# Second dense block of a two-block transformer kernel: four gate halves move from the attention's steps to the scans, and the weight ring gets two more slots

## The chip, the core and the metric

The kernel runs on one core of a Trainium2 chip. The metric is the device time of one execution in microseconds (us), the median of several runs. The engines of the core are TensorE (PE; its weight loads are PEld), VectorE (DVE), ScalarE (ACT), GpSimd (POOL) and SyncE (SP), which in this kernel issues nearly all transfers of weights. Everything is in 32-bit floats.

## The reference

256 tokens of width 1024 go through two blocks. The first is a mixer with three branches and a mixture of 32 experts. The second, in which the change lies, is:

```
def hybrid_layer(x, mem, ...):               # the second block, cut
    h = rms_norm(x, g_mix)
    u, q, k, v, qi, ki, wi, qm, gates = split(h @ w_in)
    y_ssm = s5_branch(u, ...)                # scan over 256 positions, gelu, y * sigmoid(y @ w_glu)
    y_dsa = dsa_branch(q, k, v, qi, ki, wi)  # attention on the keys that an index score picks
    y_mem = memory_branch(qm, km, vm)        # attention on the memory
    g_s, g_d, g_m = split(sigmoid(gates))    # 3 x 1024 columns of w_in
    merged = g_s*(y_ssm@w_up_ssm) + g_d*(y_dsa@w_up_dsa) + g_m*(y_mem@w_up_mem)
    x = x + merged @ w_out
    return x + hier_moe(rms_norm(x, g_ffn), ...)   # 32 experts, 2 of one group for each token
```

Each expert of `hier_moe` has three matrices, w_gate and w_up (1024 x 512) and w_down (512 x 1024), 2 MB each. The kernel reads all of them.

## The kernel before

Each engine has its program, written out in order by hand (`tensor`, `vector`, `scalar`, `sync`, `gpsimd`), and the engines meet by semaphores. `pe["name"]`, `dve["name"]`, `act["name"]` are the counts at which a named step is done.

**Weights.** The ring is a tile of seven slots of 2 MB. `fetcher` (L287 on) issues the transfers of SP: each call takes the next slot of its `lane`, waits until the weight that the slot holds has been read (`pe["free", ...]`), and issues. SP works in order, so a fetch that waits holds up all behind it. In the second dense block all weights go by the lane `d2 = (0, 1, 2)`; slots 3 to 6 hold work of the state space branch (tables, scans). Then come the 96 weights of the second mixture, in eight rounds `u` of four experts: four w_gate, four w_up, four w_down, on the lane (3, 4, 5, 6, 0, 1, 2). They wait for `sy 3` (the last product of the scans' states), and the fourth for `branch 2,0` (the output of the state space branch), since it takes slot 6.

**Gates.** The gate columns are six weights `c` of 512 columns; a gate half `i` (`gate_half`, L544 on) is four products of 128x128 by 128x512, half of the sum of one block of 128 tokens: `c = i // 4`. ACT takes a finished pair out of PSUM by a tanh (`scalar_gate`).

**The attention's steps.** `tensor_dense2` runs a loop over `s` from 0 to 13 (L958 on): `scores(s)`, `turn_p` of step s - 2, a gate half for s below 9, `values(s - 2)`. DVE does in each step the softmax, its weights, a copy of the values and one piece of `scan_step(0, s)`.

**The scans.** `driven(c)` makes the inputs of scan c (0 to 3) on PE, `scans(c)` runs it on DVE, `states(c)` multiplies its states out, `skip(c)` adds the skip term. `up(n, h)` multiplies branch n by half h of its up weight, in two parts (token blocks) in PSUM banks 0, 1 and 6, and `gated(n, h)` on DVE multiplies by the gate and frees the bank. DVE's order is scans(1), skip(0), scans(2), skip(1), gated(2,0), gated(2,1), scans(3), skip(2), gated(1,0), skip(3), gated(1,1). Behind skip(3) come the gelu (`yg`), `glu`, `branch 2,0`, up(0,0), up(0,1), the merge, its transposes (`mt2`), w_out, the norm, and the router.

**The second mixture.** `tensor_route` waits for four small loads of router weights (`s_r2`), which ACT's queue issues behind the attention's loop. `tensor_moe2` does in a round: the w_gate group (64 matmul rows of the trace, all four experts), the w_up group, spread of the round before, gather of the next, transposes (`at2`), the w_down group. A group waits for its four weights.

Work tiles lie in one large tile `ar`. GMo (offset 19024) up to 23120 holds gain vectors, masks and the memory's keys and values; 6736 to 10832 holds branch outputs and, in the mixture, selection matrices, sigmoids and outputs.

Of the kernel before, what the change touches and what calls it, by code (L numbers as in the profile page):

```python
# [8 lines left out]
ALU = mybir.AluOpType  # L9
# [5 lines left out]
NSLOT = 7  # L15
# [3 lines left out]
NE = 32  # L19
# [90 lines left out]
def build(nc, a, out, ctx):  # L110
# [11 lines left out]
    ring = ctx.enter_context(nc.sbuf_tensor("ring", [128, NSLOT * SLOT], F32))  # L122
# [22 lines left out]
    def pair(blk, u):  # L145
# [6 lines left out]
        10832, 12880, 14928, 16976, 19024, 20048, 21072, 22096, 23120, 23760, 23888)  # L152
    XV, XNV, YV = A(X, 2, 1024), A(XN, 2, 1024), A(Y, 2, 1024)
# [85 lines left out]
    TOP, NM, SM = A(10224, 2, 8), A(10240, 2), A(10242, 2)  # L239
    CT, SEL = A(10256, 256, part=(0, 32)), A(10512, 2, 32)  # L240
# [61 lines left out]
    def sync(q):  # L302
# [405 lines left out]
    def tensor_route(t, w, m, W, n, cap):  # L708
# [19 lines left out]
        w.sums(b[:, 0:32], [(upper, SEL[:, 0, :])])  # L728
        w.sums(b[:, 32:64], [(upper, SEL[:, 1, :]), (ones, SEL[:, 0, :])])
        pe["rk", m] = w.sums(b[:, 64:96], [(ones, SEL[:, 0, :]), (ones, SEL[:, 1, :])])  # L730

    def gather(t, w, m, u, lane):
        b = w.claim("swt", m, u, lane=lane)
        t.wait_ge(s_dve, dve["sel", m, u])
        for i in range(2 if m == 1 else 1):
            for tb in range(2):
                ins = t.e.transpose(b[:, TB(2 * i + tb)], SWB[:, i, tb, :], ident)  # L737
        pe["swt", m, u] = t(ins)
        t.wait_ge(s_act, act["rows", m])
        for h in range(2):  # L740
            b = w.claim("hg", m, u, h, lane=lane)
            for k in range(4):
                pe["hg", m, u, h, k] = w.sums(b[:, TB(k)], [(XNV[:, tb, TB(4 * h + k)], SB[u % 2][:, tb, :])
                                                           for tb in range(2)])

    def spread(t, w, m, u, lane):
        def block(i):
            t.wait_ge(s_act, act["yg", m, u, i])
            for tb in range(2):
                for h in range(2):  # L750
                    b = w.claim("sp", m, u, i, tb, h, lane=TL1X if i else lane)
                    pe["sp", m, u, i, tb, h] = w.sums(b[:, :], [(SWT[u % 2][:, i, TB(tb)], YG_[i][:, HALF(h)])])
# [112 lines left out]
    def tensor_dense2(t, w):  # L865
# [92 lines left out]
        for s in range(14):  # L958
# [4 lines left out]
            if s < 9:  # L963
# [36 lines left out]
        states(2)  # L1000
# [13 lines left out]
    def tensor_moe2(t, w):  # L1014
# [3 lines left out]
        for u in range(NE // 4):  # L1018
            HG, AT_ = HGB[u % 2], ATB[u % 2]
# [521 lines left out]
    def vector_ranks(v, m, cap):  # L1541
        v(v.own.tensor_scalar(SEL, CMB, 0.0, None, ALU.not_equal))
# [8 lines left out]
        v(v.own.scalar_tensor_tensor(out=RK, in0=rk, scalar=1.0, in1=SEL, op0=ALU.add, op1=ALU.mult))  # L1551
# [9 lines left out]
    def vector_select(v, m, u):  # L1561
# [14 lines left out]
        else:  # L1576

            four = [z[:, :, 4 * u:4 * u + 4].unsqueeze(3).to_broadcast([128, 2, 4, 32]) for z in (RK, CMB)]
            S = SB[u % 2].rearrange("p b (x s) -> p b x s", x=4)
            v(v.own.tensor_tensor(S, iota[:, 0:32].unsqueeze(1).unsqueeze(1).to_broadcast([128, 2, 4, 32]), four[0],  # L1580
                                  ALU.is_equal))
            k = v(v.own.tensor_tensor(SWB[:, 0].rearrange("p b (x s) -> p b x s", x=4), S, four[1], ALU.mult))
# [85 lines left out]
    def vector_dense2(v):  # L1668
# [254 lines left out]
    def vector_moe2(v):  # L1923
# [39 lines left out]
        for u in range(NE // 4):  # L1963
            sg = TM[0][:, 0:512]
# [216 lines left out]
    def scalar_gather(s, m, u, l1):  # L2181
# [4 lines left out]
        s(s.own.activation(SWT[u % 2][:, 0:n, :], ps("swt", m, u)[:, 0:256 * n].rearrange("p (i q) -> p i q", i=n),  # L2186
# [62 lines left out]
    def scalar_dense2(s):  # L2249
# [59 lines left out]
        for k in range(14):  # L2309
# [21 lines left out]
        scalar_mt(s, 2)  # L2331
        for tb in range(2):
            root_block(s, "h4", tb, dve["x3", tb, 1], YV)

    def scalar_moe2(s):
# [12 lines left out]
        for u in range(NE // 4):  # L2348
# [3 lines left out]
            act["sg2", u] = s(s.own.activation(TM[0][:, 0:512], ps("w_gate_2", u)[:, :], ACT.Sigmoid))  # L2352
# [127 lines left out]
```

## Time and profile before

| | before |
|---|---|
| median of 3 runs | 2299.73 us (2291.16 to 2302.4) |
| the profiled execution | 2301.27 us, span in the trace 2299.4 us |
| PE busy | 1850.2 us (80%), 11518 instructions |
| DVE busy | 807.2 us (35%) |
| ACT busy | 497.7 us (22%) |
| DMA | 713.56 MB, mean 310 GB/s |
| mean granted TensorE clock | 0.915 of full speed |

The first block and the first mixture take the span up to about 1475 us, the second dense block reaches to about 1820, and the second mixture is the rest. Shares are averages over all of these. The time from 2299.4 to 2301.27 lies around the traced span.

### The profile page before, as it was taken

To read this page: it belongs to the slowest core of one execution; us is meant where nothing else is said; L and a number is where in the kernel's file an instruction comes from. 1 tells how busy PE (TensorE), PEld (TensorE's weight loads), DVE (VectorE), ACT (ScalarE), POOL (GpSimd) and SP (SyncE) were. 2 spreads that over 40 slices of the span, in tenths; PEclk is the share of its full clock that TensorE was granted. 3 is DMA by queue.
4 is the path that set the end of the run, shared out by engine and by line. 5 is a ranking of instruction groups with operands and counts; after the bars stand their busy time and mean duration, and the time that the engine had idled before them with its cause. 6 is when DMAs were issued, how large, how long until landed. Compare 5 with 4: busy or idle time off the path is not lost. (4 is left out here: it accounts for less than half of the span.)

```text
span 2299.4 us, 28288 instructions
## 1 busy us (share of the span) xinstructions
PE 1850.2 (80%) x11518; PEld 837.1 (36%) x11518; DVE 807.2 (35%) x1624; ACT 497.7 (22%) x1008; POOL 77.8 (3%) x96
## 2 busy tenths in 40 slices
PE   7899998888988989779887898699977755565555
PEld 3655545333333333333333333254534422222221
DVE  2224333333433244442444433587583300000001
ACT  2031302222232133331333323321301200000000
POOL 0000000000000000000000000084000000000000
PEclk9999999899999989999999999899998877877877
DMA  7744358497797699998999999633125399999996
GB/s 270 272 162 155 120 197 326 200 380 319 323 398 309 273 424 389 423 424 341 379 424 423 424 424 421 219 128 133 40 74 219 142 428 428 428 427 428 427 427 263
DMA packets 113956, 713.56 MB, mean 310 GB/s; under 512 B 16703, under 2 KB 21006, under 8 KB 68654
## 3 DMA queue, kind: packets, MB, share of 16 engines
q1 hardware_dynamic: 105344, 704.98, 75.5%
q10 hardware_dynamic: 8398, 5.47, 0.8%
q8 instruction: 166, 2.72, 0.5%
q14 instruction: 48, 0.39, 0.1%
HBM read 709.35 MB, written 1.07 MB: 309 GB/s over the span
## 5 line engine op out<-in xcount | busy, mean ns | idle before, releaser
L795 PE MATMUL ps<-ring,ar 128*32 128x512 f32 x3072 | 380.9, 634 | 47.6 <-DMA ring<-in_w 26.1
L436 PE MATMUL ps<-ar 128*128 128x128 f32 (+5 forms) x1750 | 360.1, 363 | 36.3 <-PEq L706 15.4
L443 PE MATMUL ps<-ring,ar 128*32 128x512 f32 x1536 | 208.2, 704 | 194.1 <-DMA ring<-in_w_up 82.2
L436 PEld LDWEIGHTS ps<-ar 128*128 128x128 f32 (+2 forms) x1750 | 236.1, 201 | 161.0 <-issue 111.1
L436 PE MATMUL ps<-ring,ar 128*128 128x512 f32 (+2 forms) x624 | 268.0, 590 | 15.5 <-DVE ar L1889 8.9
L795 PEld LDWEIGHTS ps<-ring,ar 128*32 128x32 f32 x3072 | 100.2, 114 | 324.8 <-issue 277.6
L1645 DVE TENSOR_SCALAR ar<-ps 128x256 f32<-128x256 f32 x128 | 54.3, 424 | 443.5 <-PE ps L795 436.6
L806 PE MATMUL ps<-ring,ar 128*32 128x512 f32 x1536 | 175.1, 595 | 21.7 <-ACT ar L2244 21.7
L443 PEld LDWEIGHTS ps<-ring,ar 128*32 128x32 f32 x1536 | 60.0, 127 | 336.3 <-issue 335.4
L436 PEld LDWEIGHTS ps<-ring,ar 128*128 128x128 f32 x624 | 120.6, 195 | 155.9 <-issue 137.6
L551 PE MATMUL ps<-ring,ar 128*128 128x512 f32 x384 | 172.4, 598 | 0.0
L1591 DVE TENSOR_TENSOR ar<-ps,ar 128x512 f32<-128x512 f32 x180 | 124.5, 692 | 100.2 <-PE ps L436 91.4
L2216 ACT ACTIVATE ar<-ps 64x512 f32<-64x512 f32 x256 | 151.5, 592 | 26.1 <-PE ps L806 14.3
L2210 ACT ACTIVATE ar<-ar 128x256 f32<-128x256 f32 x128 | 53.3, 417 | 385.2 <-DVE ar L1645 382.4
L1653 DVE TENSOR_TENSOR ar<-ar 128x256 f32<-128x256 f32 x128 | 79.3, 620 | 119.8 <-ACT ar L2210 109.7
L2244 ACT ACTIVATE ar<-ps 128x256 f32<-128x256 f32 x128 | 49.2, 384 | 239.5 <-PE ps L816 218.0
L551 PEld LDWEIGHTS ps<-ring,ar 128*128 128x128 f32 x384 | 71.2, 192 | 78.1 <-issue 77.7
L1966 DVE TENSOR_TENSOR ar<-ps,ar 128x512 f32<-128x512 f32 x8 | 5.5, 692 | 266.7 <-ACT ar L2352 266.7
L788 PE MATMUL ps<-ar 32*32 32x512 f32 x384 | 53.7, 622 | 49.5 <-ACT ar L2216 19.3
L806 PEld LDWEIGHTS ps<-ring,ar 128*32 128x32 f32 x1536 | 46.4, 109 | 114.6 <-issue 90.2
L2193 ACT ACTIVATE ar<-ps 128x512 f32<-128x512 f32 x80 | 47.8, 597 | 104.1 <-PE ps L436 104.1
L2186 ACT ACTIVATE ar<-ps 128x512 f32<-128x512 f32 (+1 forms) x40 | 22.2, 555 | 179.7 <-PE ps L737 177.6
(392 smaller groups left out, 1285.9 us busy)
## 6 DMA issues: line engine op xcount, KB each, us to landing
ring<-in_w SPq DMA_DIRECT2D x192, 2048.0 KB, 18.4
ring<-in_w_gate SPq DMA_DIRECT2D x32, 2048.0 KB, 17.8
ring<-in_w_up SPq DMA_DIRECT2D x32, 2048.0 KB, 16.7
ring<-in_w_down SPq DMA_DIRECT2D x32, 2048.0 KB, 16.0
ring<-in_w_in SPq DMA_DIRECT2D x21, 2048.0 KB, 8.7
ring<-in_w_ada SPq DMA_DIRECT2D x12, 2048.0 KB, 8.8
ring<-in_w_out SPq DMA_DIRECT2D x4, 2048.0 KB, 8.1
ring<-in_w_branch SPq DMA_DIRECT2D x6, 1024.0 KB, 5.0
```

The costliest lines, as they stand in the source:

```text
L436: ins = self.t.e.matmul(o, l, r, start=(i == 0), stop=(i == len(pairs) - 1))
L443: ins = self.t.e.matmul(b[32 * i:32 * i + 32, :], l, r, start=(k == 0), stop=(k == len(steps) - 1))
L551: ins = t.e.matmul(b[:, :], HV[:, k, TB(tb)], W[:, k, :], start=(k == 0), stop=(k == 7))
L788: e.matmul(b[32 * s:32 * s + 32, :], pick, B1R[:, HALF(s)], start=True, stop=False)
L795: ins = e.matmul(b[32 * s:32 * s + 32, :], HG[:, 2 * c + r, 32 * n:32 * n + 32], W[:, r, HALF(s)], start=False, stop=(c == 3 and r == 1))
L806: ins = e.matmul(b[64 * h + 32 * r:64 * h + 32 * r + 32, :], AT_[:, 2 * s + r, 32 * n:32 * n + 32], W[:, s % 2, r, HALF(h)], start=(s == 0 ...
L1591: v(v.own.tensor_tensor(o, ps("sp", m, u, i, tb, h)[:, :], o, ALU.add))
L1645: dve["glu", u, n] = v(v.own.tensor_scalar(glu, b[:, 0:512:2], 7.0, None, ALU.min))
L1653: dve["ac", u, n] = v(v.own.tensor_tensor(o, lin.rearrange("p (q r) -> p q r", r=2), sg.rearrange("p (q r) -> p q r", r=2), ALU.mult))
L2210: act["sg", u, n] = s(s.own.activation(M[:, 512:768], M[:, 0:256], ACT.Sigmoid, scale=1.702))
L2216: k = s(s.own.activation(YG_[n // 2][64 * (n % 2):64 * (n % 2) + 64, HALF(h)], ps("l2", u, n)[64 * h:64 * h + 64, :], ACT.Copy))
L2244: m = s(s.own.activation(o, ps("at", u, k)[:, 256 * i:256 * i + 256].rearrange("p (r s n) -> p r s n", r=2, s=4), ACT.Copy))
```

## The change

Three things go together. Four gate halves (16 to 19) leave steps 5 to 8 of the loop, and all of 16 to 23 stand between the scans' products. The weights of the block and of the mixture get nine slots: slot 7 is GMo to 23120, slot 8 is 6736 to 10832 of `ar`. For that the mixture's small tiles move, AT and SWT get homes of their own (AT2 is single), the lanes are set weight by weight, and SP's order changes: the up weights go out behind `pv 11`, w_out behind three w_gate. The router's loads go behind the transposes of the merge on ACT's queue, as their tile now lies in a gate's place, and gated(1,0) goes behind skip(3).

```diff
-NSLOT = 7
+NSLOT = 9
+RING = 7
@@ def RG_(i, off, *shape):
+        if i >= RING:
+            return A(MORE[i - RING] + off, *shape)
@@
+    MORE = (GMo, 6736)
@@ tiles of the mixture
-    AC2 = A(4096, 512)
+    AT2, AC2, YG2 = A(2048, 4, 128), A(3072, 512), A(3584, 1024)
+    SB2 = [A(4608 + 256 * i, 2, 128) for i in range(2)]
+    SWB2 = A(5120, 1, 2, 128)
+    SWT2 = [A(5376 + 256 * i, 1, 256) for i in range(2)]
+    SG2 = A(5888, 512)
@@
-    W36, B36 = A(9216, 8, 36), A(9504, 36)
+    W36, B36 = A(2512, 8, 36), A(2800, 36)
@@ def sync(q):
         for c in range(6):
             fetch(("gate", 2, c), w_in2[:, :, 1988 + 512 * c:2500 + 512 * c], 8, 512, lane=d2)
-        for n in (2, 1):
-            for h in range(2):
-                up(n, h)
-        fetch(("glu",), kpn(a["w_glu_2"][0]), 4, 512, lane=d2)
-        for h in range(2):
-            up(0, h)
-        for h in range(2):
-            fetch(("wo", 2, h), kpn(a["w_out_2"][0])[:, :, HALF(h)], 8, 512, lane=d2)
+        up(2, 0, (1,))
+        q.wait_ge(s_pe, pe["pv", 2, 11])
+        up(2, 1, (7,))
+        up(1, 0, (2,))
+        up(1, 1, (0,))
+        fetch(("glu",), kpn(a["w_glu_2"][0]), 4, 512, lane=(1,))
+        up(0, 0, (7,))
+        up(0, 1, (2,))
+        units = [(nm, u, i) for u in range(NE // 4) for nm in ("w_gate_2", "w_up_2", "w_down_2") for i in range(4)]
+        lanes = (3, 4, 5, 6, 8, 7, 2, 0, 1)
         q.wait_ge(s_pe, pe["sy", 3])
-        for u in range(NE // 4):
-            for nm, r in (("w_gate_2", 8), ("w_up_2", 8), ("w_down_2", 4)):
-                for i in range(4):
-                    if (u, nm, i) == (0, "w_gate_2", 3):
-                        q.wait_ge(s_dve, dve["branch", 2, 0])
-                    fetch((nm, u, i), a[nm][0, 4 * u + i].rearrange("(p r) n -> p r n", r=r), r, SLOT // r,
-                          lane=(3, 4, 5, 6, 0, 1, 2))
+        for k, (nm, u, i) in enumerate(units):
+            if k == 3:
+                out2(0, (0,))
+                out2(1, (1,))
+                q.wait_ge(s_dve, dve["branch", 2, 0])
+            if k == 4:
+                q.wait_ge(s_pe, pe["up", 0, 1, 1])
+            r = 4 if nm == "w_down_2" else 8
+            fetch((nm, u, i), a[nm][0, 4 * u + i].rearrange("(p r) n -> p r n", r=r), r, SLOT // r,
+                  lane=(lanes[k % 9],))
@@ def tensor_dense2(t, w): the loop over s
-            if s < 9:
+            if s < 5:
                 gate_half(t, w, 2, 11 + s)
@@ and behind it
         driven(1)
         states(0)
-        gate_half(t, w, 2, 20)
-        gate_half(t, w, 2, 21)
+        for i in (16, 17):
+            gate_half(t, w, 2, i)
         driven(2)
-        gate_half(t, w, 2, 22)
-        gate_half(t, w, 2, 23)
+        for i in (18, 19, 20, 21):
+            gate_half(t, w, 2, i)
+        states(1)
+        driven(3)
+        for i in (22, 23):
+            gate_half(t, w, 2, i)
         t.wait_ge(s_dve, dve["branch", 2, 2])
         up(2, 0, side)
-        states(1)
-        driven(3)
         up(2, 1, side)
+        states(2)
         t.wait_ge(s_dve, dve["branch", 2, 1])
         up(1, 0, side)
-        states(2)
         states(3)
         up(1, 1, side)
@@ def vector_dense2(v):
         scans(3)
         skip(2)
-        gated(1, 0)
         skip(3)
         dve["tc"] = v.n
+        gated(1, 0)
         gated(1, 1)
@@ def scalar_dense2(s): in the loop over k, and behind it
-            if k < 10 and k % 2 == 0:
+            if k < 5 and k % 2 == 0:
                 scalar_gate(s, 2, 5 + k // 2)
-        e.dma_start(W36[:, :, 0:4], kpn(a["w_group_2"][0])).then_inc(s_r2, 16)
...
-        got["rt", 2] = 64
-        for g in range(10, 12):
+        for g in range(8, 12):
             scalar_gate(s, 2, g)
...
         scalar_mt(s, 2)
+        e.dma_start(W36[:, :, 0:4], kpn(a["w_group_2"][0])).then_inc(s_r2, 16)
...
+        got["rt", 2] = 64
@@ def scalar_moe2(s):
-            if u > 1:
-                s.wait_ge(s_pe, pe["l2_2", u - 2, 1])
-            act["at2", u] = s(s.own.activation(ATB[u % 2][:, 0:4, :],
+            if u > 0:
+                s.wait_ge(s_pe, pe["l2_2", u - 1, 1])
+            act["at2", u] = s(s.own.activation(AT2,
```

## Rows read from the trace of the kernel before

**Rows 1.** The page: DMA's busy tenths and GB/s in 40 equal slices.

```profile
DMA  7744358497797699998999999633125399999996
GB/s 270 272 162 155 120 197 326 200 380 319 323 398 309 273 424 389 423 424 341 379 424 423 424 424 421 219 128 133 40 74 219 142 428 428 428 427 428 427 427 263
```

**Rows 2.** Chain of waits in order of time: start, us, piece.

```profile
1828.95 7.12 PE ps L443 x64
1836.08 7.57 DMA ring<-in_w_up
...
2277.45 8.77 PE ps L443 x64
```

**Rows 3.** A window: busy us by engine, TensorE clock, DMA share, GB/s.

```profile
1860.00:2260.00 400.00, 222.93 (x1568) 85.48 (x1572) 32.84 (x49) 25.60 (x45) 0.00 (x0) 0.78 1.01 427
```

**Rows 4.** Timeline of SP's issues: start, us, tensor, count.

```profile
1758.51 2.21 SPq L296 DMA_DIRECT2D ring<-in_w_gate  x4
1801.56 34.85 SPq L296 DMA_DIRECT2D ring<-in_w_up  x4
```

**Rows 5.** Timeline of PE, attention steps (L936 starts a step, L551 gate half).

```profile
1620.50 0.70 PE L936 MATMUL ps<-ar 64*128 64x256 f32 x4
...
1622.54 3.60 PE L551 MATMUL ps<-ring,ar 128*128 128x512 f32 x8
...
1645.41 0.70 PE L936 MATMUL ps<-ar 64*128 64x256 f32 x4
...
1648.39 0.66 PE L954 MATMUL ps<-ar 128*64 128x128 f32 x8 [0.78 <-DVE small L1395]
1648.98 0.70 PE L936 MATMUL ps<-ar 64*128 64x256 f32 x4
...
1654.15 0.60 PE L568 MATMUL ps<-ar 128*128 128x128 f32 x4
```

**Rows 6.** Timeline of PE, last attention step to states(3).

```profile
1661.74 2.11 PE L436 MATMUL ps<-ring 32*128 32x256 f32 x16
1663.78 3.22 PE L443 MATMUL ps<-ring 128*32 128x256 f32 x32
1666.93 7.13 PE L551 MATMUL ps<-ring,ar 128*128 128x512 f32 x16
...
1704.59 13.64 PE L436 MATMUL ps<-ring,ar 128*128 128x512 f32 x24 [8.90 <-DVE ar L1889]
...
1731.98 3.25 PE L443 MATMUL ps<-ar,ring 128*32 128x256 f32 x32 [11.89 <-DVE ring L1880]
```

**Rows 7.** Timeline of DVE, weights of step 10, gated(2,.), next turn_in.

```profile
1651.98 0.74 DVE L1397 TENSOR_SCALAR ar<-ar,small 128x256 f32<-128x256 f32 x2
...
1703.84 2.23 DVE L1889 SCALAR_TENSOR_TENSOR ar<-ar,ps 128x512 f32<-128x512 f32 x3
1711.40 0.69 DVE L1889 SCALAR_TENSOR_TENSOR ar<-ar,ps 128x512 f32<-128x512 f32 x1 [5.33 <-PE ps L436]
1712.12 0.69 DVE L1823 TENSOR_TENSOR ar<-ps,ring 128x512 f32<-128x512 f32 x1
```

**Rows 8.** Windows at the end of the attention steps.

```profile
1656.00:1660.00 4.00, 2.24 (x20) 1.29 (x16) 3.52 (x9) 1.26 (x5) 0.00 (x0) 0.95 0.00 0
1656.00:1672.00 16.00, 13.55 (x88) 7.07 (x85) 13.43 (x21) 1.80 (x5) 0.00 (x0) 0.79 0.10 12
```

**Rows 9.** DMA issues: KB of each, median us to landing.

```profile
ring<-in_w_out SPq DMA_DIRECT2D x4, 2048.0 KB, 8.1
...
ar<-in_w_router ACTq DMA_DIRECT2D x1, 128.0 KB, 15.9
...
ar<-in_w_expert ACTq DMA_DIRECT2D x1, 128.0 KB, 2.6
```

**Rows 10.** Timeline of PE, w_out and the router's sums.

```profile
1771.22 22.56 PE L436 MATMUL ps<-ring,ar 128*128 128x512 f32 x48 [2.28 <-ACT ar L2106]
...
1801.37 1.87 PE L436 MATMUL ps<-ar 128*128 128x36 f32 x16
```

More of the change, by code:

```diff
@@ L235, in build @@
     TM = [A(9216 + 768 * i, 768) for i in range(2)]
[L236 removed]
+    AT2, AC2, YG2 = A(2048, 4, 128), A(3072, 512), A(3584, 1024)
[3 more added lines that the diff above has]
+    SG2 = A(5888, 512)
     B1R = A(HT, 2048, part=(0, 32))
     L, E, E2 = A(10000, 2, 32), A(10064, 2, 40), A(10144, 2, 40)
[L239 to L240 removed]
+    TOP, NM, SM = A(10224, 2, 8), small[:, 104:106], small[:, 106:108]
+    CT, SEL = A(10256, 256, part=(0, 32)), [A(10512, 2, 32), A(2872, 2, 32)]
     AT = [A(2048 * i, 8, 256) for i in range(2)]
@@ L727, in tensor_route @@
         t.wait_ge(s_c2, 16)
-        w.sums(b[:, 0:32], [(upper, SEL[:, 0, :])])
-        w.sums(b[:, 32:64], [(upper, SEL[:, 1, :]), (ones, SEL[:, 0, :])])
-        pe["rk", m] = w.sums(b[:, 64:96], [(ones, SEL[:, 0, :]), (ones, SEL[:, 1, :])])
+        s0, s1 = (SEL[m - 1][:, tb, :] for tb in range(2))
+        w.sums(b[:, 0:32], [(upper, s0)])
+        w.sums(b[:, 32:64], [(upper, s1), (ones, s0)])
+        pe["rk", m] = w.sums(b[:, 64:96], [(ones, s0), (ones, s1)])
     def gather(t, w, m, u, lane):
@@ L742, in gather @@
             for k in range(4):
-                pe["hg", m, u, h, k] = w.sums(b[:, TB(k)], [(XNV[:, tb, TB(4 * h + k)], SB[u % 2][:, tb, :])
+                pe["hg", m, u, h, k] = w.sums(b[:, TB(k)], [(XNV[:, tb, TB(4 * h + k)], (SB, SB2)[m - 1][u % 2][:, tb, :])
                                                            for tb in range(2)])
@@ L751, in block @@
                     b = w.claim("sp", m, u, i, tb, h, lane=TL1X if i else lane)
-                    pe["sp", m, u, i, tb, h] = w.sums(b[:, :], [(SWT[u % 2][:, i, TB(tb)], YG_[i][:, HALF(h)])])
+                    pe["sp", m, u, i, tb, h] = w.sums(b[:, :], [((SWT, SWT2)[m - 1][u % 2][:, i, TB(tb)],
+                                                            (YG_[i] if m == 1 else YG2)[:, HALF(h)])])
         block(0)
@@ L1018, in tensor_moe2 @@
         for u in range(NE // 4):
-            HG, AT_ = HGB[u % 2], ATB[u % 2]
+            HG, AT_ = HGB[u % 2], AT2
             rows = [slice(32 * i, 32 * i + 32) for i in range(4)]
@@ L1541, in vector_ranks @@
     def vector_ranks(v, m, cap):
-        v(v.own.tensor_scalar(SEL, CMB, 0.0, None, ALU.not_equal))
+        v(v.own.tensor_scalar(SEL[m - 1], CMB, 0.0, None, ALU.not_equal))
         dve["sel", m] = v.n
@@ L1550, in vector_ranks @@
         v(v.own.tensor_tensor(CO_, CO_, CMB, ALU.mult))
-        v(v.own.scalar_tensor_tensor(out=RK, in0=rk, scalar=1.0, in1=SEL, op0=ALU.add, op1=ALU.mult))
+        v(v.own.scalar_tensor_tensor(out=RK, in0=rk, scalar=1.0, in1=SEL[m - 1], op0=ALU.add, op1=ALU.mult))
         v(v.own.tensor_scalar(RK, RK, -1.0, None, ALU.add))
@@ L1578, in vector_select @@
             four = [z[:, :, 4 * u:4 * u + 4].unsqueeze(3).to_broadcast([128, 2, 4, 32]) for z in (RK, CMB)]
-            S = SB[u % 2].rearrange("p b (x s) -> p b x s", x=4)
+            S = SB2[u % 2].rearrange("p b (x s) -> p b x s", x=4)
             v(v.own.tensor_tensor(S, iota[:, 0:32].unsqueeze(1).unsqueeze(1).to_broadcast([128, 2, 4, 32]), four[0],
                                   ALU.is_equal))
-            k = v(v.own.tensor_tensor(SWB[:, 0].rearrange("p b (x s) -> p b x s", x=4), S, four[1], ALU.mult))
+            k = v(v.own.tensor_tensor(SWB2[:, 0].rearrange("p b (x s) -> p b x s", x=4), S, four[1], ALU.mult))
         dve["sel", m, u] = k
@@ L2185, in scalar_gather @@
             s.wait_ge(s_pe, pe["sp", m, u - 2, n - 1, 1, 1])
-        s(s.own.activation(SWT[u % 2][:, 0:n, :], ps("swt", m, u)[:, 0:256 * n].rearrange("p (i q) -> p i q", i=n),
+        s(s.own.activation((SWT, SWT2)[m - 1][u % 2][:, 0:n, :], ps("swt", m, u)[:, 0:256 * n].rearrange("p (i q) -> p i q", i=n),
                            ACT.Copy))
@@ L2351, in scalar_moe2 @@
                 s.wait_ge(s_dve, dve["ac2", u - 1])
-            act["sg2", u] = s(s.own.activation(TM[0][:, 0:512], ps("w_gate_2", u)[:, :], ACT.Sigmoid))
+            act["sg2", u] = s(s.own.activation(SG2, ps("w_gate_2", u)[:, :], ACT.Sigmoid))
             if u + 1 < NE // 4:
@@ L2364, in scalar_moe2 @@
                 s.wait_ge(s_pe, pe["l2_2", u, h])
-                n = s(s.own.activation(YG_[0][:, HALF(h)], ps("l2_2", u, h)[:, :], ACT.Copy))
+                n = s(s.own.activation(YG2[:, HALF(h)], ps("l2_2", u, h)[:, :], ACT.Copy))
                 read["l2_2", u, h] = s.mark()
```

26 lines of the change are left out of this document (14 added, 12 removed).

## The prediction, made before the changed kernel ran

> **What bounds the kernel now.** I read the page first, then the chain of waits from 1450 us on, then the timeline of each engine through the second dense block. The page's last fifteen slices [rows 1] fall into two parts: from slice 26 to 32 the DMA rate is low and uneven, and from slice 33 it stands at 427 to 428 GB/s. The chain [rows 2] shows what the second part is: in the second mixture every group of products waits for a weight (32 experts, three matrices of 2 MB, 96 transfers), so the end of the kernel is the time at which the stream of weights becomes continuous, plus the bytes that are left, plus a tail. One long window [rows 3] gives the rate, 427 GB/s, so one transfer of 2,097,152 bytes costs 4.91 us.
>
> When does the stream become continuous? The SP queue's timeline [rows 4] tells: four w_gate transfers go out at 1758.5, three w_up at 1801.6 as w_out and the last up weights leave slots 0 to 2, and then nothing, because seven slots are full. The eighth (w_up, expert 3) needs slot 3, which the first w_gate group reads. That group starts at 1828.95 and ends at 1836.0 [rows 2], and at 1836.08 SP goes on. From there 96 - 7 = 89 transfers are left, and the last group starts at 2277.45 [rows 2]: 441.4 us, of which 89 x 4.91 = 437.0 are bytes and 4.4 are start and landing. Then 22.0 us of tail to 2299.4. So two things move the end: the time of the first w_gate group (call it G), which the dense block's chain sets, and how many transfers are left at G.
>
> **Two more slots.** After the change nine slots are full at G: the lanes (3,4,5,6,8,7,2,0,1) take w_gate 0-3, w_up 0-3 and w_down 0. The last two go to slots 0 and 1 when the two w_out halves are read, in before's times at about 1794 and 1801.5 [rows 10], and 4.91 us each fit well before 1828.95. Left at G: 87. The gain is 2 x 4.91 = 9.8 us. It isn't given back later: with nine slots and 3 to 5 free per group the issues run further ahead than now, and now the window already shows a DMA share of 1.01 [rows 3]. The w_up group, which waits 7.57 us for its fourth weight today, starts at once; that only frees slots earlier. Bounds: nothing (if the stream slowed) and 9.8.
>
> A rule to weigh against this: the stream runs at 427 GB/s in the trace [rows 3]. The Trainium skill (DMA: Bandwidth & Descriptors, Where 436 GB/s comes from) says that HBM to SBUF is held to about 358 GB/s per core; by that rule, as an estimate, a transfer would cost 5.86 us and two slots would be worth 11.7. The trace decides, and it doesn't agree.
>
> **Four gate halves leave the attention's steps.** Loop s runs scores, turn_p, one gate half, values. From step 5 to 8 it takes 1620.50 to 1645.41, 24.91 us, with PE busy throughout [rows 5]: PE bound. Steps 9 and 10 have no gate half and take 3.57 us each (1645.41, 1648.98 and so on); of that 0.78 is PE waiting for ACT's copy of the turned weights, which a gate half of 3.44 us covers today [rows 5]. DVE's work in such a step fits: the weights that turn_p reads at 1654.15 are done at 1652.72 [rows 5, 7]. So steps 5 to 8 become 4 x 3.57, plus 0.39 in step 5 whose values (u = 3) are the longer kind: 14.7 us. Gain 10.2 us. ACT loses two gate evictions in the loop, which nobody waits for.
>
> **Where they land.** After the steps PE now runs driven(1), states(0), halves 16, 17, driven(2), 18 to 21, states(1), driven(3), 22, 23, up(2,0), up(2,1). Today DVE's scans bound this stretch, and PE has slack: it idles 8.9 us before 1704.59 [rows 6]. In before's times: 1666.93 when the first half starts; two halves 7.0 each pair [rows 6]. 1666.93 + 7.07 + 1.1 (driven) + 13.94 + 1.9 (states) + 1.1 + 6.97 = 1699.0; up(2,0) two parts to 1705.9, up(2,1) two parts to 1712.9. driven(2) keeps its place, so scans(2) isn't late. DVE reaches gated(2,0) at 1703.84 as now, follows PE's four parts, and the last ends at 1712.9 + 0.2 + 0.7 = 1713.8; scans(3) starts then, against 1712.12 now [rows 7]. Today DVE also waits here (5.33 us before 1711.40), because the fourth part needs a bank that DVE frees late and then runs at half clock after PE's idleness, 6.8 us instead of 3.5 [rows 6, 7]. So the 14 us that arrive cost only 1.7. Bounds: -0.6 if PE's slow start at 1661.74 (half clock, [rows 8], about 2.3 us) is gone, and 1.7 + 3.4 = 5.1 if one more half-clock stretch falls into this packed run (the one around 1660 is 6.7 us long: a mean of 0.79 over 16 us, [rows 8]).
>
> From scans(3) on, the order hardly changes. PE waits for DVE again (11.9 us before states(3) today [rows 6], some 11 after). gated(1,0) goes behind skip(3); skip(3) waits for states(3) in either case, and up(1,1)'s second part needs the bank that gated(1,0) frees only 3.4 us after its first has begun. Nought. G moves by -10.2 + 1.7 = -8.5.
>
> **Waits added on SP.** All weights of the block now queue behind pv 11; the first, up(2,1), lands some 5 us later and is wanted 40 us later. up(1,0), up(1,1), glu and up(0,.) each go out when their slot's user is done and land at least 8 us ahead of use. out2(0), out2(1) stand behind three w_gate: with wait sy 3 over at 1735.2 (states(3) ends, [rows 6]) and slot 1 free after up(1,1) and glu, 7 us each, at 1749.2, the fifth transfer lands near 1737.4 + 5 x 4.91 + 2 = 1764, before w_out is wanted at 1771.2 [rows 10]; cover 7 us. If it shared the engines with all nine transfers in flight it would land at 1783.6 and cost 12.4. Today's w_out takes 8.1 us with four w_gate issued right behind it [rows 9], so they are served in order. Nought.
>
> The four router loads move on the ACT queue from 1660 to behind the merged transposes at 1771.2 [rows 10] and are wanted at 1801.4: cover 30 us. The expert load takes 2.6 us in a quiet stretch, the router of the first mixture, as large, 15.9 in traffic [rows 9]. Their issue (2 us on ACT) lies ahead of a wait for w_out. Nought. Single AT2 and moved tiles: their waits are on groups long done. Nought.
>
> **Sum.** -9.8 - 8.5 = -18.3. The profiled execution takes 2301.27 (span 2299.4), so 2283.0; it lies 1.5 above the median of the runs shown.
>
> **Rivals.**
> (a) The clock. Thinner steps leave PE idle 22% of the time, and the clock falls to 1.2 GHz at about 1660, after steps 12 and 13 in which PE was busy 2.24 of 4 us [rows 8]. Against it: steps 9 to 11, as thin as the new ones will be, ran at 2.4 GHz. With 2.79 us of PE work in 3.57, a half-clock stretch of 6.7 us covers 1.05 steps instead of 1.9 and so costs 3.0 in the steps, and 3.4 more if one follows in the packed run: -11.9, 2289.4. The Trainium skill (TensorE: Matmul & The Clock Gate, A second HAM failure mode) warns that short idle gaps between groups make the clock oscillate; steps 9 to 11 don't show it, the end of the loop does.
> (b) Only the slots pay: the 10.2 come back in the scans, since the halves are on PE's path there. For it: PE's spare time before 1704.59 is 8.9 and 14 arrive. 2291.5.
> (c) Only the chain pays: transfers ahead of G don't shorten the stream. 2292.8.
> (d) Slower: the stream itself slows, with more transfers in flight and two slots in the work tile that every engine uses. It decides from 18.3 / 87 = 0.21 us per transfer, 409 GB/s. Slices of the first mixture at 389 [rows 1] would mean 5.39, +41.8, so 2324.8. Against: slices 33 to 39 hold 427 while PE, DVE and ACT work.
> (e) The change does nothing measurable: both gains are eaten by waits that the profile doesn't show; 2301.
>
> **Chances.** Forecast 0.58, (a) 0.14, (b) 0.09, (c) 0.07, (d) 0.05, (e) 0.07. The range: the forecast's own bounds are 2280.7 and 2289; (a) to (c) reach 2292.8, and the runs of before spread 8.6 us below their median, so I take 2274 to 2293, which leaves out (d), (e) and little else. A measurement here tells about 0.5% (11.5 us) from no change. Faster by more than that: the forecast and half of (a), with a little of the rest: 0.70. Same 0.25, slower 0.05.
>
> **What would show it.** Steps 5 to 8 at 3.6 us each; scans(3) starting 8 to 9 us earlier than 1712.1; the first w_gate group at about 1820.5, and the w_up group right behind it without a wait; nine transfers issued before it; DMA at 427 GB/s from 1828 to the last group at about 2259; tail 22. It would be wrong if w_out or the router's sums wait for a DMA, if the clock is down in steps 5 to 8, or if the window of the stream shows less than 427.

## The result

| | before | after |
|---|---|---|
| median, first measurement | 2295.44 us (4 runs, 2288.95 to 2302.4) | 2268.61 us (4 runs, 2264.78 to 2276.13) |
| ratio | | 0.9897 (0.9867 to 0.9927) |
| the profiled execution | 2301.27, span 2299.4 | 2265.11, span 2263.2 |
| PE busy | 1850.2 | 1843.9 |
| DVE busy | 807.2 | 807.2 |
| mean granted clock | 0.915 | 0.918 |

The changed kernel is faster by 1.0%, some 24 us. The forecast was 2283.0 with a range of 2274 to 2293: the direction was right, the time lies 5 us below the range. A later comparison with more runs (`after_again`, below) gives 0.9915. The two profiled executions differ by 36 us, twice what was forecast, and the first question is where the rest comes from.

The page of after, the two lines that answer to [rows 1]:

```profile
DMA  7744348498798699999999999733128299999995
GB/s 275 273 161 155 130 170 338 187 406 329 312 399 346 244 425 399 423 424 376 403 425 423 424 424 421 263 116 124 63 87 326 98 428 427 428 428 428 427 428 248
```

The stream of 427 to 428 GB/s is there again from slice 33 on. Slice 31 holds 326 GB/s where before had 219: more of the mixture's transfers go out ahead of the first w_gate group.

The chain of after, the start of the first w_gate group and of the last group, as in [rows 2], and two windows of the stream, as in [rows 3]:

```profile
1801.10 13.94 PE ps L460 x128
...
2239.74 10.06 PE ps L460 x64
```

```profile
1860.00:2240.00 380.00, 220.81 (x1508) 85.38 (x1512) 35.09 (x51) 24.39 (x43) 0.00 (x0) 0.78 1.00 424
1850.00:2220.00 370.00, 211.96 (x1476) 81.86 (x1468) 32.81 (x49) 24.39 (x43) 0.00 (x0) 0.78 1.01 428
```

The first w_gate group and its w_up group now stand in one piece of 128: the wait of 7.57 us between them is gone. From G, the start of that group, to the last group it is 438.6 us (448.5 before). The tail is 23.5 us (21.9). The stream kept its rate: the first window reads 424 GB/s since it takes in the last 4 us ahead of the last group, in which the transfers run out; the second, which stops before that, reads 428. What is left of the time from G to the last group when 4.91 us for each transfer are taken off is the same as before, 438.6 - 87 x 4.91 = 11.4 against 448.5 - 89 x 4.91 = 11.5.

SP's issues in after, to be set beside [rows 4]:

```profile
1709.13 1.30 SPq L306 DMA_DIRECT2D ring<-in_w_gate  x3
1716.57 7.28 SPq L306 DMA_DIRECT2D ring<-in_w_out  x2
1725.15 4.43 SPq L306 DMA_DIRECT2D ring<-in_w_gate  x1
1739.21 0.81 SPq L306 DMA_DIRECT2D ar<-in_w_up  x2
1740.06 26.62 SPq L306 DMA_DIRECT2D ring<-in_w_up  x2
1774.10 35.41 SPq L306 DMA_DIRECT2D ring<-in_w_down  x4
```

Nine mixture weights leave before G = 1801.10: three w_gate, a fourth, three w_up (two of them to `ar`), the fourth w_up at 1766.4, and w_down 0 at 1774.10. The row of w_down is merged: its other three follow at 1808.2, when the w_gate group is done.

The attention's steps 5 to 8 of after, as in [rows 5]; each row starts a step:

```profile
1602.63 0.70 PE L955 MATMUL ps<-ar 64*128 64x256 f32 x4
...
1606.67 0.70 PE L955 MATMUL ps<-ar 64*128 64x256 f32 x4
...
1610.24 0.70 PE L955 MATMUL ps<-ar 64*128 64x256 f32 x4
...
1613.80 0.70 PE L955 MATMUL ps<-ar 64*128 64x256 f32 x4
...
1617.37 0.70 PE L955 MATMUL ps<-ar 64*128 64x256 f32 x4
```

The steps take 4.04, 3.57, 3.56 and 3.57 us, together 14.7, as forecast (24.9 before).

PE from the last attention step to states(3), as in [rows 6], then DVE at the end of the packed run, as in [rows 7]:

```profile
1633.93 2.11 PE L453 MATMUL ps<-ring 32*128 32x256 f32 x16
1635.97 2.99 PE L460 MATMUL ps<-ring 128*32 128x256 f32 x32
1638.89 7.13 PE L568 MATMUL ps<-ring,ar 128*128 128x512 f32 x16
...
1647.05 14.00 PE L568 MATMUL ps<-ring,ar 128*128 128x512 f32 x32
1660.98 1.94 PE L460 MATMUL ps<-ar,ring 128*32 128x256 f32 x32
...
1677.78 7.03 PE L453 MATMUL ps<-ar 128*128 128x512 f32 x16
...
1705.43 3.64 PE L460 MATMUL ps<-ar,ring 128*32 128x256 f32 x32 [11.70 <-DVE ring L1901]
```

```profile
1681.47 0.69 DVE L1910 SCALAR_TENSOR_TENSOR ar<-ar,ps 128x512 f32<-128x512 f32 x1 [2.80 <-PE ps L453]
1684.85 0.69 DVE L1910 SCALAR_TENSOR_TENSOR ar<-ar,ps 128x512 f32<-128x512 f32 x1 [2.69 <-PE ps L453]
1685.57 0.69 DVE L1844 TENSOR_TENSOR ar<-ps,ring 128x512 f32<-128x512 f32 x1
```

The halves 16 and 17 stand at 1638.89, 18 to 21 at 1647.05. scans(3) starts at 1685.57 behind the fourth gated(2,.). PE still waits 11.7 us before states(3).

Some waits were feared and didn't come. The loads as in [rows 9], and PE's w_out and router sums as in [rows 10]:

```profile
ring<-in_w_out SPq DMA_DIRECT2D x4, 2048.0 KB, 11.9
...
ar<-in_w_expert ACTq DMA_DIRECT2D x1, 128.0 KB, 12.6
```

```profile
1745.46 20.87 PE L453 MATMUL ps<-ring,ar 128*128 128x512 f32 x48 [2.27 <-ACT ar L2127]
...
1773.90 1.87 PE L453 MATMUL ps<-ar 128*128 128x36 f32 x16
```

The product with w_out waits for ACT, as before. The x4 of the w_out row takes in the first block's two. The second block's two stand behind three w_gate, and the five landed some 5 us apart; w_out took 16.4 and 14.9 us, and the later one landed at 1738.4, 7.1 us before the products with w_out start: the cover of 7 us that the prediction gave. The router's expert load took 12.6 us in traffic, not 2.6; the last of the four loads landed at 1759.2, 14.7 us before the router's sums at 1773.90.

### Where the 36 us between the two profiles lie

I cut each trace at the same events: the first projection of the second block (PE's 64 matmul rows on w_in_2, at 1485.87 in before and 1468.02 in after), which ends the first part; the start of the attention's steps ("loop"), as a distance behind that projection; states(0); the starts of scans(2) and scans(3); states(3); G; and the last group. All numbers are us. Two stretches are left out of the table: states(0) to scans(2) is 20.1 in every profile, and scans(3) to states(3) is 19.9 in all but late_gated (23.3) and late_gated2 (20.1). The last column is the total time in the trace's clock record at half clock between 424 us (the start of the first mixture) and the first projection.

| kernel | first part | loop of steps starts | loop to states(0) | scans(2) to scans(3) | states(3) to G | G to last group | tail | half clock in the first mixture |
|---|---|---|---|---|---|---|---|---|
| before | 1485.9 | +108.2 | 69.7 | 28.2 | 97.0 | 448.5 | 21.9 | 105.8 |
| aa_before | 1469.1 | +112.3 | 69.7 | 28.2 | 96.9 | 448.5 | 21.9 | 85.1 |
| slots_only | 1476.2 | +112.4 | 69.7 | 28.2 | 97.0 | 438.6 | 22.1 | 91.8 |
| gates_only | 1478.9 | +108.6 | 58.6 | 28.7 | 96.8 | 448.6 | 21.9 | 92.2 |
| after | 1468.0 | +108.2 | 59.7 | 29.5 | 95.7 | 438.6 | 23.5 | 88.7 |
| after_again | 1481.0 | +113.3 | 58.6 | 28.7 | 96.8 | 438.5 | 21.9 | 98.3 |
| eight_slots | 1473.4 | +115.4 | 59.9 | 28.8 | 95.3 | 443.7 | 22.5 | 90.2 |
| late_wout | 1475.4 | +112.1 | 59.7 | 29.5 | 105.8 | 438.6 | 21.7 | 99.0 |
| halves_cut | 1466.2 | +112.2 | 59.6 | 32.1 | 96.4 | 438.8 | 21.8 | 88.6 |
| halves_cut_2 | 1478.4 | +112.1 | 59.7 | 32.1 | 96.4 | 438.7 | 21.7 | 98.9 |
| late_gated | 1477.3 | +108.6 | 58.6 | 20.0 | 95.5 | 438.9 | 23.1 | 105.8 |
| late_gated2 | 1476.4 | +112.5 | 59.6 | 20.0 | 95.2 | 438.7 | 23.2 | 84.8 |

Between before and after the first part, whose code the change doesn't touch, is 17.9 us shorter and the second part, the rest of the span, 18.3 us shorter (813.5 to 795.2). In the first part the two are within 1.2 us of each other up to about 465 us; from there the distance grows in jumps. Here is the largest, of 6.6 us, a stretch of the first mixture with the same 202 matmul rows, first in before, then in after:

```profile
1003.60:1043.60 40.00, 32.66 (x202) 10.82 (x204) 11.90 (x25) 9.73 (x19) 0.00 (x0) 0.79 1.00 422
```

```profile
996.20:1029.60 33.40, 29.38 (x202) 10.17 (x201) 11.91 (x25) 9.72 (x19) 0.00 (x0) 0.90 1.00 422
```

The stretch takes 40.0 and 33.4 us, at a mean clock of 0.79 and 0.90. PE is busy for 32.66 and 29.38 of it, so half of the 6.6 us is the same rows at 1.2 GHz for longer, and half is more waiting of PE, whose cause is not shown.

### The profile page after: what moved, and what is told of

The parts are those of the page before. It is cut to its first block and busy times, and to the rows that moved or that the text cites. A ratio compares the mean times of both kernels' runs of the same rounds, so it can differ in the third digit from the quotient of the medians.

```text
span 2263.2 us, 28291 instructions
## 1 busy us (share of the span) xinstructions
PE 1843.9 (81%) x11518; PEld 834.9 (37%) x11518; DVE 807.2 (36%) x1624; ACT 497.1 (22%) x1008; POOL 77.6 (3%) x96
## 5 line engine op out<-in xcount | busy, mean ns | idle before, releaser
L453 PE MATMUL ps<-ar 128*128 128x128 f32 (+5 forms) x1782 | 369.6, 364 | 36.0 <-PEq L723 14.1
L453 PE MATMUL ps<-ring,ar 128*128 128x512 f32 (+2 forms) x592 | 249.5, 581 | 4.9 <-ACT ar L2127 2.6
L825 PE MATMUL ps<-ring,ar 128*32 128x512 f32 x1536 | 175.4, 595 | 21.7 <-ACT ar L2265 21.7
L453 PEld LDWEIGHTS ps<-ring,ar 128*128 128x128 f32 x592 | 113.2, 193 | 134.9 <-issue 128.4
L1612 DVE TENSOR_TENSOR ar<-ps,ar 128x512 f32<-128x512 f32 x180 | 124.4, 691 | 96.9 <-PE ps L453 87.3
L460 PE MATMUL ps<-ar 128*32 128x512 f32 x352 | 111.5, 696 | 26.4 <-DMA ring<-in_w_up 20.0
L568 PEld LDWEIGHTS ps<-ring,ar 128*128 128x128 f32 x384 | 71.4, 192 | 79.9 <-issue 79.5
L807 PE MATMUL ps<-ar 32*32 32x512 f32 x384 | 51.2, 597 | 41.4 <-DVE ar L1667 14.7
## 6 DMA issues: line engine op xcount, KB each, us to landing
ar<-in_w_up SPq DMA_DIRECT2D x8, 2048.0 KB, 25.7
```

The source lines that it names most:

```text
L453: ins = self.t.e.matmul(o, l, r, start=(i == 0), stop=(i == len(pairs) - 1))
L460: ins = self.t.e.matmul(b[32 * i:32 * i + 32, :], l, r, start=(k == 0), stop=(k == len(steps) - 1))
L568: ins = t.e.matmul(b[:, :], HV[:, k, TB(tb)], W[:, k, :], start=(k == 0), stop=(k == 7))
L807: e.matmul(b[32 * s:32 * s + 32, :], pick, B1R[:, HALF(s)], start=True, stop=False)
L825: ins = e.matmul(b[64 * h + 32 * r:64 * h + 32 * r + 32, :], AT_[:, 2 * s + r, 32 * n:32 * n + 32], W[:, s % 2, r, HALF(h)], start=(s == 0 ...
L1612: v(v.own.tensor_tensor(o, ps("sp", m, u, i, tb, h)[:, :], o, ALU.add))
```

## The experiments

The question after the result was whether the first part is a matter of the execution or of the change, and whether the two halves of the change are worth what the sum says. All kernels of a comparison ran beside the kernel before on the same chip. eight_slots, late_wout and the two runs of halves_cut are one execution each and are read from their profiles alone.

### The kernel before, once more

Nothing is edited.

> The kernel before, unchanged, profiled once more. The first part is the time from the start of the trace to the first projection of the second block (1485.87 us in the profile of before, 1468.02 in that of after); the second part is the rest of the span (813.5 and 795.2). Theory A (the 17.9 us by which the first parts differ are spread between executions, not the change): the ratio is 1 within its interval, the second part is 813.5 plus or minus 4, and the first part falls anywhere from 1465 to 1492. Theory B (the change shortens the first part too): the first part is 1486 plus or minus 3 again.

Measured: ratio 1.0001 (0.9981 to 1.0022), ten runs from 2281.71 to 2302.41. The first part of its profile is 1469.1, 16.8 less than in the first profile of the same kernel and 1.1 more than in after. The second part is 817.5, at the very edge of the 813.5 plus or minus 4 (the 4 us lie ahead of the loop, second column of the table; why is not shown). Theory A holds and B falls: the same program gives either length of the first part.

### The changed kernel, once more

Nothing is edited.

> The changed kernel, profiled once more and timed against before in five rounds. Theory A: second part 795.2 plus or minus 4, first part anywhere from 1465 to 1492, and the difference of the two kernels' times near -18 us (ratio 0.992). Theory B: first part 1468 plus or minus 3, difference -27 us or more (ratio 0.988 or less).

Measured: 2276.81 us (six runs, 2268.15 to 2280.87) against 2292.13 for before (27 runs), ratio 0.9915 (0.9888 to 0.9942), which is -19.5 us with a wide interval (-25.7 to -13.3). First part 1481.0, second part 797.9. Both are as theory A says. The first ratio, 0.9897, came from four runs against four, and the two intervals overlap; that it took in some of the spread is likely, not shown.

### The slots without the gates

```diff
-            if s < 5:
+            if s < 9:
                 gate_half(t, w, 2, 11 + s)
...
-        skip(3)
-        dve["tc"] = v.n
-        gated(1, 0)
+        gated(1, 0)
+        skip(3)
+        dve["tc"] = v.n
```

and the products between the scans and ACT's evictions in the order of before.

> The changed kernel with the gate halves, the products and gated(1,0) back where before has them: nine slots, SP's new order and the moved tiles alone. My sum: two transfers less behind the first w_gate group, -9.8 us in the second part (803.7), the first w_gate group as far behind the first projection as in before (343.1 us), loop steps 5 to 8 at 6.15 us. Rival (the slots pay nothing by themselves, since the stream ends when it ends): 813.5.

The chain, the first w_gate group and the last group:

```profile
1823.47 13.94 PE ps L460 x128
...
2262.04 8.62 PE ps L460 x64
```

Measured: ratio 0.9955 (0.9932 to 0.9979), -10.3 us. G to last group 438.6, 9.9 less than before. The distance from the first projection to G is 347.2, which is aa_before's 347.1 and not the 343.1 of the first profile; the 4 us lie ahead of the loop (the second column), where nothing is edited. For the same reason the second part is 807.9, not the 803.7 expected. The rival, no gain by slots alone, is out.

### The gates without the slots

```diff
-            if s < 9:
+            if s < 5:
                 gate_half(t, w, 2, 11 + s)
...
+        for i in (16, 17):
+            gate_half(t, w, 2, i)
         driven(2)
+        for i in (18, 19, 20, 21):
+            gate_half(t, w, 2, i)
```

and the rest of PE's, ACT's and DVE's order as the change has it; seven slots and SP as before.

> The kernel before with its seven slots, its lanes and SP's order, and only the order of PE, ACT and DVE of the change. My sum: the first w_gate group 8.5 us nearer to the first projection (334.6 us), second part 805.0. Rival (the halves' time comes back in the scans): 343 and 813.5. If the parts add, this gain and that of slots_only make the 18.3 us between the profiles of before and after.

```profile
1811.58 7.12 PE ps L443 x64
...
2260.14 8.65 PE ps L443 x64
```

Measured: ratio 0.9971 (0.9950 to 0.9991), -6.6 us. Loop to states(0) 58.6 instead of 69.7, scans(2) to scans(3) 28.7 instead of 28.2, G to last group unchanged at 448.6. From the first projection to G it is 332.7, the second part 803.1, each 1.9 us less than expected: the loop gives 0.9 us more than forecast, with the clock up at its end in this profile, and the packed run costs 1.2 less. The rival, that the halves' time comes back in the scans, is out. The stages of the two partial kernels add up to those of the whole: -9.9 from the slots and -10.6 from the gates, -20.5, which is also what after_again shows against before from the start of the loop on (-20.6); by the ratios it is -10.3 and -6.6, together -17. The -6.6 is a wide figure (-11.5 to -2.1), and the stages' -10.6 lies in it.

### Eight slots

```diff
-        lanes = (3, 4, 5, 6, 8, 7, 2, 0, 1)
+        lanes = (3, 4, 5, 6, 8, 2, 0, 1)
...
-                  lane=(lanes[k % 9],))
+                  lane=(lanes[k % 8],))
```

> The changed kernel with slot 7 left out of the mixture's lanes (eight slots there, slot 7 still serves two up weights). If a slot pays one transfer of 4.91 us behind the first w_gate group, the time from the first w_gate group to the last group is 443.5 us, halfway between 448.5 (seven slots) and 438.5 (nine). Rival (the gain comes from the w_up group that no longer waits, or from SP's order, not from the number of slots): 438.5 or 448.5.

The chain, then SP's issues:

```profile
1812.75 13.94 PE ps L460 x128
...
2256.50 9.06 PE ps L460 x64
```

```profile
1778.04 8.07 SPq L306 DMA_DIRECT2D ring<-in_w_up  x2
1819.89 1.85 SPq L306 DMA_DIRECT2D ring<-in_w_down  x4
```

Measured: 443.7 us from G to the last group. All four w_up are there at G, so PE does 128 rows in one piece as with nine slots, but w_down 0 isn't: its row begins at 1819.89. With seven, eight and nine slots the time is 448.5, 443.7 and 438.6, so a slot is worth one transfer (4.8 and 5.1 us against 4.91), and the vanished wait of 7.57 us before the w_up group is worth nothing of its own.

### w_out issued later

```diff
             if k == 3:
-                out2(0, (0,))
-                out2(1, (1,))
                 q.wait_ge(s_dve, dve["branch", 2, 0])
             if k == 4:
                 q.wait_ge(s_pe, pe["up", 0, 1, 1])
+                out2(0, (0,))
+                out2(1, (1,))
```

> The changed kernel with the two w_out transfers issued behind w_gate 3 and the wait for up(0,1,1), ahead of w_up 0. They then land 2 + 9.8 + 2 = 13.8 us behind up(0,1,1), 7.4 us after the moment at which w_out's products start now (6.4 us behind it): the first w_gate group comes 7 to 8 us later, 104 instead of 96.8 behind states(3). If the cover of 7 us that the prediction gave them was really there, this is what its loss costs. Rival (w_out already sets the pace today, or never does): no change.

PE's timeline at w_out:

```profile
1764.61 22.99 PE L453 MATMUL ps<-ring,ar 128*128 128x512 f32 x48 [10.13 <-DMA ring<-in_w_out]
```

Measured: PE waits 10.13 us for w_out, of which 2.3 are the wait for ACT that is there anyway; states(3) to G takes 105.8, 9.0 to 10.1 more. The wait beyond ACT's is 7.9 us, against the 7.4 expected, so the cover was real. The other 2.1 us are the products with w_out themselves, 22.99 us against 20.87 in after, with PE at half clock after the wait (44.4 us at half clock between scans(3) and G, 34.1 in after).

### What the four halves cost in the packed run

This kernel leaves out three of the four products in each of the halves 16 to 19.

```diff
-        for k in range(4 * half, 4 * half + 4):
+        ks = range(4 * half, 4 * half + 4) if (blk, c) != (2, 4) else (7 * half,)
+        for k in ks:
```

> The changed kernel with one product instead of four in each of gate halves 16 to 19 (three quarters of these sums are left out), so PE has 10.5 us less in the packed run. By my account of that stretch the end of the run is then set by the bank that DVE frees late, not by PE's work: scans(3) starts 25.2 us behind scans(2) if the clock stays up, 28 if it falls during the wait, against 28.7 to 29.5 with the halves; so the four halves together cost 0.5 to 4 us there. Rival (the halves are on the path with all their time): 10.5 us less, 18 to 19.

PE's timeline from the halves 18 to 21 on:

```profile
1645.27 8.85 PE L569 MATMUL ps<-ring,ar 128*128 128x512 f32 x20
1658.25 3.25 PE L460 MATMUL ps<-ar,ring 128*32 128x256 f32 x32 [4.13 <-DVE ring L1902]
1661.43 1.14 PE L453 MATMUL ps<-ring 32*128 32x256 f32 x8
1662.72 1.13 PE L453 MATMUL ps<-ring 32*128 32x256 f32 x4 [0.15 <-DVE ring L1846]
1664.24 1.97 PE L453 MATMUL ps<-ring 32*128 32x256 f32 x4 [0.40 <-DVE ring L1846]
1666.14 9.64 PE L569 MATMUL ps<-ring,ar 128*128 128x512 f32 x16
```

Measured: scans(3) starts 32.1 us behind scans(2), later than with all the work. Both expectations were wrong. PE, with less to do, reaches states(1) early and waits 4.13 us for DVE (its PSUM bank is freed by skip(0), L1902), then catches up with DVE at the banks of driven(3) (16 rows from 1661.43 to 1666.14, 1.1 us in after), and is at half clock meanwhile: states(1) takes 3.25 us instead of 1.93, and halves 22 and 23 take 9.6 instead of 7.1. I had followed only the bank of the fourth up part and not these two waits.

> halves_cut once more. Its first look had scans(3) 32.1 us behind scans(2), later than with all the work (28.7 to 29.5), with PE at half clock for 12.6 us of the run behind states(0). If that belongs to the kernel (PE waits 4 us for scans(1) ahead of states(1), and the clock falls around that), this look shows 28 to 33 again and more than 6 us at half clock; if it was the chance of one execution, 25.2 and the clock up.

A window of the second run over the same piece:

```profile
1667.00:1688.00 21.00, 17.03 (x65) 8.32 (x66) 19.82 (x25) 0.06 (x1) 0.00 (x0) 0.76 0.00 1
```

Measured: 32.1 again, the clock at 0.76 in that window. It belongs to the kernel. The account closes: PE starts states(1) 0.04 us behind scans(2), not 4.9 as in after, and still ends 2.6 us later, so 7.4 us are lost behind it. They are 1.3 in states(1), 3.6 in driven(3) and 2.5 in the halves 22 and 23. In after the halves 16 to 19 therefore fill time in which PE would wait for DVE, and the clock stays up there. That the stretch as a whole is longer without them is shown twice; how much of the 7.4 us is clock and how much waiting is an estimate (3.8 us of slower rows, 3.6 in driven(3), in which there is some of both).

### gated behind scans(3)

```diff
-        side = (0, 1, 6)
+        side = (0, 1, 6, 2, 3, 4, 5)
...
         skip(1)
+        scans(3)
         gated(2, 0)
         gated(2, 1)
-        scans(3)
         skip(2)
         skip(3)
```

> The changed kernel with gated(2,0) and gated(2,1) moved on DVE from ahead of scans(3) to behind it, and up's products on seven PSUM banks (0, 1, 6, 2 to 5) instead of three, so that no product waits for gated. If scans(3) waits today for PE's packed run, it now starts 20.0 us behind scans(2), as scans(2) does behind scans(1), instead of 28.7 to 29.5: 9 us less to the first w_gate group; PE then has 2 instead of 11.7 us of idle time before states(3), so up to 3 us more may come from a clock that stays up. Second part 784 to 789 instead of 795 to 798; faster than the changed kernel by 9 to 12 us. Rival: the four gated stand between states(3) and skip(3) and give back 3 us, or states(3) waits for up(1,0): 4 to 6 us.

DVE's timeline at the end of scans(3):

```profile
1702.74 1.22 DVE L1867 TENSOR_TENSOR ar<-ar,ring 128x1024 f32<-128x1024 f32 x1
1704.10 3.09 DVE L1910 SCALAR_TENSOR_TENSOR ar<-ar,ps 128x512 f32<-128x512 f32 x4
1707.31 0.48 DVE L1901 SCALAR_TENSOR_TENSOR ring<-ring,ar,ps 128x256 f32<-128x256 f32 x1
```

Measured: 2266.27 us (six runs), ratio to before 0.9878 (0.9849 to 0.9908). scans(3) follows scans(2) in 20.0 us, 9 less. The second part is 788.2, in the expected 784 to 789, but the distance to the two profiles of the changed kernel (7.0 and 9.7) takes in what differs ahead of the loop. From the start of the loop to G it is 217.6 us against 224.9 and 224.2, so 7 us less. That is under the 9 to 12 expected, and the rival is why: states(3) starts 23.3 us behind scans(3) instead of 19.9. skip(2), which frees its bank, stands behind the four gated (3.09 us).

```diff
         scans(3)
+        skip(2)
         gated(2, 0)
         gated(2, 1)
-        skip(2)
         skip(3)
```

> late_gated with skip(2) ahead of gated(2,0) and gated(2,1) on DVE. In late_gated states(3) began 23.3 us behind the start of scans(3) instead of 19.9, since its PSUM bank is freed by skip(2), which stood behind the four gated (3.1 us). With skip(2) first it begins at 19.9 again, and the four gated run while PE does states(3): 3.4 us less, the first w_gate group 323 us behind the first projection (326.2 in late_gated), second part 783 to 786. Rival (skip(3) then waits for the gated, 3.1 us against the 2 to 4 us of states(3)): up to 1 us of the 3.4 is lost.

DVE and PE:

```profile
1706.75 1.23 DVE L1867 TENSOR_TENSOR ar<-ar,ring 128x1024 f32<-128x1024 f32 x1
1708.09 0.48 DVE L1901 SCALAR_TENSOR_TENSOR ring<-ring,ar,ps 128x256 f32<-128x256 f32 x1
1708.68 2.92 DVE L1910 SCALAR_TENSOR_TENSOR ar<-ar,ps 128x512 f32<-128x512 f32 x4
1712.16 0.48 DVE L1901 SCALAR_TENSOR_TENSOR ring<-ring,ar,ps 128x256 f32<-128x256 f32 x1 [0.56 <-PE ps L460]
```

```profile
1708.72 3.39 PE L460 MATMUL ps<-ar,ring 128*32 128x256 f32 x32 [2.30 <-DVE ring L1901]
```

Measured: 2267.86 us, ratio 0.9871 (0.9843 to 0.9898). states(3) starts 20.1 behind scans(3), and skip(3) waits only 0.56 us. From the start of the loop to G it takes 215.0 us (327.5 less the 112.5 ahead of the loop), against 217.6 in late_gated, 224.9 and 224.2 in the changed kernel and 234.8 in before. The expected 323 to G, counted from the first projection, was missed by the 4 us ahead of the loop; so were the 783 to 786 for the second part (789.4). In the timed runs the two kernels can't be told apart. Both have a ratio to before that is lower than the changed kernel's 0.9915 by 0.4%, with intervals that still overlap; by the stages they are faster than it by 7 to 10 us.

## Why the prediction was right or wrong

**The level was wrong.** The step that failed is the last one of the sum: "The profiled execution takes 2301.27 (span 2299.4), so 2283.0; it lies 1.5 above the median of the runs shown." It put a difference of -18.3 on the time of one execution. That execution was a slow one: 27 later runs of the same kernel have a median of 2292.13, 9.1 less. With that under it the sum gives 2273.8. What is left of the miss, 5.2 us, is no more than the spread of the four runs of the changed kernel (2264.78 to 2276.13). The ten runs of it in the two comparisons have a median of 2272.8, and the second comparison alone, 2276.81, lies inside the range.

The profiles show where the level came from. Of the 12 the profiled execution of before has the longest first part, 1485.9 (the others 1466.2 to 1481.0; the middle of the 12 is 1476.3). Ahead of the loop it is, the other way, one of the four short ones (108.2, the middle is 112.2).

The range had the same fault. It took the spread of three runs as reaching 8.6 us downward and set its low end at 2274, while single runs of one kernel spread over 20 us (2281.71 to 2302.41 for ten of before).

**The slots: right, in mechanism and size.** -9.8 was forecast; 448.5 to 438.6 is -9.9, and eight slots give 443.7. The stream kept its rate (427 GB/s before, 428 in after) and the gain wasn't given back. Rival (d), a slower stream, is refuted by the same rate. Rival (c), that transfers ahead of G don't shorten the stream, is out by slots_only. By an estimate from the 358 GB/s of the Trainium skill (DMA: Bandwidth & Descriptors, Where 436 GB/s comes from) this term would have been -11.7, and the trace doesn't agree with that one.

**The steps: right.** -10.2 was forecast for steps 5 to 8, and they went from 24.9 to 14.7 us. Over the whole loop it is -9.9 in after and -11.1 in the three profiles whose clock stayed up over the end of the loop (gates_only, after_again, late_gated). The 3.57 us of steps 9 and 10 carried over to steps 5 to 8 to the hundredth.

**The packed run: right size, reason incomplete.** +1.7 was forecast, +1.3 and +0.5 measured. But halves_cut shows that the stretch isn't PE's work plus one bank: with 10.5 us less it took 32.1 instead of 28.7 to 29.5. The forecast added up PE's work and never asked whether PE would wait for skip(0)'s bank and for DVE's turn_in; it came out right since the halves fill just that time. That was luck.

**From scans(3) to G: nearly nothing, as said.** The part behind states(3) went from 97.0 to 95.7 in after, and to 96.8 in after_again and gates_only. The -1.3 is mostly in w_out's products: 22.56 us in before [rows 10] and 20.87 in after. The waits that I costed at nothing had their cover: w_out, whose loss of cover costs 9 to 10 us in late_wout, and the router's loads, which landed 14.7 us before their use.

**The sum.** Loop -9.9, packed run +1.3, states(3) to G -1.3, slots -9.9, tail +1.6: before rounding -18.3 between the two profiles, against -18.3. That it fits so well is partly luck. The -1.3 and the tail's +1.6 were not in the sum and cancel; the tail varies from 21.7 to 23.5 over the profiles. The second profile of the changed kernel gives -20.6 from the start of the loop on. Ahead of the loop, where nothing is edited, the two first profiles are alike, but others are up to 7 us longer there.

**Rival (a), the clock.** In every profile with the change the steps 5 to 8 start at the same distances to 0.1 us, and the clock record has no time at half clock in them. Over the whole loop it has 0 to 6.0 us with the change and 4.2 to 4.3 without it. Rival (b), the gain of the steps coming back in the scans, is refuted by gates_only. Rival (e), no measurable change, is out by the interval of either ratio. Of the three outcomes the one that came is faster by over 0.5%, to which 0.70 was given.

## What to carry to other kernels

When the end of a kernel is a continuous stream of transfers, count the transfers that are left when it becomes continuous. Here each slot filled before that moment was worth one transfer, and a wait inside the stream that went away was worth nothing. A change of order is best priced from a piece of the same loop that already runs without the moved work. Before adding a difference to a level, ask how much the level itself spreads between executions: here the forecast difference was right to within 2.3 us in both profiles of the changed kernel, and the absolute time was outside the range.

## What the runs showed of the hardware

The time of one program spreads by 20 us (0.9%) between executions: ten runs of before went from 2281.71 to 2302.41. In these profiles part of the spread is TensorE's clock. In the stretch above, of the same 202 matmul rows, PE was busy for 29.38 us at a mean clock of 0.90 and for 32.66 at 0.79. Of before's two profiles the one with more half-clock time in the first mixture (105.8 against 85.1 us) has the longer first part (1485.9 against 1469.1). Over all 12 the two go together only loosely: late_gated has 105.8 us at half clock too and a first part of 1477.3. That half clock costs nothing where PE would wait anyway may be the reason; it is not shown. Why one execution has more of it than another isn't shown either.

Taking work away from PE can make a stage longer. halves_cut leaves 10.5 us of products out and its stage grew by 3 us, twice, with the clock down around and after a wait of 4.13 us.

The packed run shows the other side. Its 36 us of back-to-back products, from 1650 on in after, ran at 2.4 GHz:

```profile
1650.00:1686.00 36.00, 36.00 (x146) 16.11 (x148) 27.79 (x34) 3.07 (x4) 0.00 (x0) 1.00 0.26 89
```

In before PE idles for 8.9 us ahead of 1704.59, and the clock falls in that wait; the first up part behind it took 6.8 us instead of 3.5 [rows 6].

```profile
1696.00:1712.00 16.00, 7.42 (x10) 3.11 (x11) 10.12 (x13) 0.00 (x0) 0.00 (x0) 0.68 0.00 1
```

The Trainium skill (TensorE: Matmul & The Clock Gate, Loop structure matters more than you think) shows a loop in which a long wait for a DMA before the products makes TensorE go cold. The traces agree, and here the waits were for DVE: 8.9 us in before, and 4.13 us in halves_cut.
